# Where the conditioning sums stand in a feed-forward unit, and two attention turns moved among the value chunks

## The reference, cut to what matters

```python
def swiglu_ffn(x, w_in, w_out):                       # ffn1, ffn2, ffn3: hidden width 2816
    gate, up = jnp.split(x @ w_in, 2, axis=-1)
    return (jax.nn.silu(gate) * up) @ w_out

mod = c_act @ w_ada[i] + b_ada[i]                     # i = 0, 1; w_ada[i] is 1024 x 6144
sh_a, sc_a, g_a, sh_f, sc_f, g_f = jnp.split(mod, 6, axis=-1)

def _neighborhood_attention(h, w_qkv, rpb, w_o):      # 16 heads of 64, 4 rows of 64 columns
    q, k, v = ...                                     # h @ w_qkv
    s = jnp.einsum('bqhd,bkqjhd->bhqkj', q_r, k_g) + bias
    p = jax.nn.softmax(...)
    return jnp.einsum('bhqkj,bkqjhd->bqhd', p, v_g)   # then @ w_o
```

## Time and profile before

| | us |
|---|---|
| median of 3 runs | 1566.19 (1565.66 to 1570.25) |
| the profiled execution | 1566.99 |
| its span in the trace | 1565.2 |
| PE busy | 1511.3 (97%) |
| DVE busy | 1156.7 (74%) |
| ACT busy | 875.7 (56%) |
| POOL busy | 83.3 (5%) |

### The profile page before, as it was taken

One profiled execution on the slowest core, in us unless ns is written; L12 is line 12 of the kernel. 1 busy time (PEld: TensorE's weight loads), 2 busy tenths in 40 slices (PEclk: granted clock), 3 DMA queues, 4 the chain that ended last, 5 costly groups with the idle time before them and its releaser, 6 DMA issues.

```text
span 1565.2 us, 21487 instructions
## 1 busy us (share of the span) xinstructions
PE 1511.3 (97%) x8712; PEld 1256.7 (80%) x8712; DVE 1156.7 (74%) x1351; ACT 875.7 (56%) x1064; POOL 83.3 (5%) x90
## 2 busy tenths in 40 slices
PE   7999999989999999999999999999999999999998
PEld 6888879987778878967788876788888888888886
DVE  5767669765677767466767754579989888998997
ACT  5444457553534445365344444567777777777775
POOL 0100003220122200000000001000000000000000
PEclk9999999999999999999999999999999999999999
DMA  8887734222678764335877720359998998998993
GB/s 350 305 300 274 268 108 139 78 78 107 259 303 321 301 244 162 135 109 231 300 292 281 258 96 1 111 214 397 332 351 329 347 368 314 364 348 315 374 340 134
DMA packets 56788, 388.80 MB, mean 248 GB/s; under 512 B 10144, under 2 KB 10480, under 8 KB 12784
## 3 DMA queue, kind: packets, MB, share of 16 engines
q1 hardware_dynamic: 55280, 378.79, 64.4%
q0 software_dynamic: 1408, 8.60, 1.5%
HBM read 386.31 MB, written 1.06 MB: 247 GB/s over the span
## 4 chain that ended last, share of the span: by engine, by line
PE 85%; DVE 9%; ACT 4%; DMA 2%; issue 1%; DVEq 0%; ACTq 0%
PE bank L346 23%; PE bank L348 23%; PE bank L347 23%; PE bank L1369 4%; DVE sb_wlo L273 2%; DVE sb_ada_raw L786 2%; PE bank L1940 1%; DMA sb_ada_raw<-in_ada 1%; PE bank L591 1%; ACT sb_whi L269 1%; PE bank L748 1%; PE bank L2178 1%; PE bank L2140 1%; PE bank L2485 1%; PE bank L2519 1%
## 5 line engine op out<-in xcount | busy, mean ns | idle before, releaser
L273 DVE TENSOR_TENSOR sb_wlo<-sb_raw,sb_whi 128x2048 fp32r<-128x2048 f32 x135 | 311.4, 2308 | 114.5 <-ACT sb_whi L269 114.4
L269 ACT ACTIVATE sb_whi<-sb_raw 128x2048 fp32r<-128x2048 f32 x135 | 258.6, 1917 | 241.5 <-PE bank L348 227.5
L346 PE MATMUL bank<-sb_whi,sb_xhi 128*128 128x512 f32 (+1 forms) x736 | 280.5, 381 | 5.6 <-DVE sb_wlo L273 4.1
L347 PE MATMUL bank<-sb_wlo,sb_xhi 128*128 128x512 f32 (+1 forms) x736 | 275.6, 374 | 0.0
L348 PE MATMUL bank<-sb_whi,sb_xlo 128*128 128x512 f32 (+1 forms) x736 | 275.6, 374 | 0.0
L2449 DVE TENSOR_TENSOR sb_wlo<-sb_raw,sb_whi 128x2048 fp32r<-128x2048 f32 x84 | 190.9, 2286 | 12.6 <-ACT sb_whi L2443 11.9
L346 PE MATMUL bank<-sb_whi,sb_slots_hi 128*128 128x512 f32 x448 | 181.2, 404 | 0.0
L348 PE MATMUL bank<-sb_whi,sb_slots_lo 128*128 128x512 f32 x448 | 176.2, 393 | 0.0
L347 PE MATMUL bank<-sb_wlo,sb_slots_hi 128*128 128x512 f32 x448 | 175.5, 392 | 0.0
L2443 ACT ACTIVATE sb_whi<-sb_raw 128x2048 fp32r<-128x2048 f32 x84 | 160.9, 1917 | 25.5 <-PE bank L348 25.3
L346 PEld LDWEIGHTS bank<-sb_whi,sb_xhi 128*128 128x128 f32 x736 | 139.3, 189 | 33.1 <-DVE sb_wlo L273 6.2
(11 more groups left out here) (455 smaller groups left out, 2519.4 us busy)
## 6 DMA issues: line engine op xcount, KB each, us to landing
sb_raw<-in_ffn SPq DMA_DIRECT2D x98, 1024.0 KB, 5.8
sb_raw<-in_moe SPq DMA_DIRECT2D x86, 1024.0 KB, 6.4
sb_ada_raw<-in_ada SPq DMA_DIRECT2D x32, 1536.0 KB, 8.4
sb_cst<-in_moe SPq DMA_DIRECT2D x28, 1024.0 KB, 6.8
sb_xn<-in_moe SPq DMA_DIRECT2D x27, 1024.0 KB, 6.8
sb_ada_raw<-in_moe SPq DMA_DIRECT2D x27, 1024.0 KB, 6.7
sb_raw<-in_w_in SPq DMA_DIRECT2D x13, 1024.0 KB, 4.8
sb_raw<-in_na_qk SPq DMA_DIRECT2D x8, 1024.0 KB, 5.0
```

The costliest lines, as they stand in the source:

```text
L269: e.activation(whi[s][:, :], raw[s][:, :], ACT.Copy).then_inc(s_hi[s], 1)
L273: e.tensor_tensor(wlo[s][:, :], raw[s][:, :], whi[s][:, :], ALU.subtract).then_inc(s_lo[s], 1)
L346: e.matmul(dst, wh, xh, start=first, stop=False, skip_group_check=skip)
L347: e.matmul(dst, wh, xl, start=False, stop=False, skip_group_check=skip)
```

## The change

In `ffn`: the sums of piece j leave unit j and are made in unit j+1, one tile between `low` of B and `low` of A, two between `low` of A and `low` of C. On SP the transfer of piece j moves behind the loads of B and A. In the last units `low` of the last B chunk goes ahead of `v_hlo`, and the last piece of a feed-forward of 11 pieces is summed, all three tiles, behind its last `v_hlo`. In the attention, `attend` becomes a generator, and its turns 0 and 1 are taken behind value chunks 9 and 10; `meet` becomes `release` (no engine waits), the value products wait for all marks of `linear` instead, and the bank of the spread sums alternates the other way round (`turn`).

```diff
             def sp_unit(e, j):
                 if also is not None:
                     also(e, j)
+                load(e, B_, b0[B_] + j + 1, w[j + 1, 1])
+                load(e, A_, b0[A_] + j + 2, w[j + 2, 0])
                 if has_ada(j):
                     sp_ada(e, j)
-                load(e, B_, b0[B_] + j + 1, w[j + 1, 1])
-                load(e, A_, b0[A_] + j + 2, w[j + 2, 0])
                 load(e, C_, b0[C_] + j + 1, w[j + 1, 2])
@@ dve_unit
                 low(e, B_, b0[B_] + j)
+                if has_ada(j - 1):
+                    v_ada(e, j - 1, (0,))
                 low(e, A_, b0[A_] + j + 1)
-                if has_ada(j):
-                    v_ada(e, j, (0, 1))
+                if has_ada(j - 1):
+                    v_ada(e, j - 1, (1, 2))
                 low(e, C_, b0[C_] + j)
-                if has_ada(j):
-                    v_ada(e, j, (2,))
@@ sp_ffn
                 units(e, sp_unit)
+                load(e, B_, b0[B_] + n - 1, w[n - 1, 1])
+                load(e, A_, b0[A_] + n, w[n - 1, 2])
                 if has_ada(n - 2):
                     sp_ada(e, n - 2)
-                load(e, B_, b0[B_] + n - 1, w[n - 1, 1])
-                load(e, A_, b0[A_] + n, w[n - 1, 2])
                 if has_ada(n - 1):
                     sp_ada(e, n - 1)
@@ dve_ffn
-                if has_ada(0):
-                    v_ada(e, 0, range(ADA_T))
                 units(e, dve_unit)
                 dve_unit(e, n - 2)
...
+                    v_mult_rows(e, n - 2)
+                    low(e, B_, b0[B_] + n - 1)
+                    v_hlo(e, n - 2)
+                if has_ada(n - 2):
+                    v_ada(e, n - 2, (0,))
                 low(e, A_, b0[A_] + n)
+                if has_ada(n - 2):
+                    v_ada(e, n - 2, (1, 2))
                 (v_mult if rolled else v_mult_rows)(e, n - 1)
                 v_hlo(e, n - 1)
                 if has_ada(n - 1):
-                    v_ada(e, n - 1, (2,))
+                    v_ada(e, n - 1, range(ADA_T))
@@ attend
-    turn = lambda b, n: bank[b + n % 2][:, 0:T] if prepare is None else ...
+    turn = lambda b, n: bank[b + (n + b // 6) % 2][:, 0:T] if prepare is None else ...
@@ neighbourhood
+        def between():
+            calls.append(None)
+            if len(calls) in (2 * 9 + 2, 2 * 10 + 2):
+                next(turns)
```

More of the change, by code:

```diff
@@ L685, in ffn @@
                 tally["table"] += 1
-            has_ada = lambda j: isinstance(j, int) and j < ada_n
+            has_ada = lambda j: ada_n > 0 and isinstance(j, int) and j < ada_n
             def hbuf(j):
@@ L927, in dve_ffn @@
                 low(e, A_, b0[A_] + 1)
-                if has_ada(0):
-                    v_ada(e, 0, range(ADA_T))
                 units(e, dve_unit)
                 dve_unit(e, n - 2)
[L932 to L936, removed]
+                if rolled:
+                    v_mult(e, n - 2)
+                    v_hlo(e, n - 2)
+                    low(e, B_, b0[B_] + n - 1)
+                else:
+                    v_mult_rows(e, n - 2)
+                    low(e, B_, b0[B_] + n - 1)
+                    v_hlo(e, n - 2)
+                if has_ada(n - 2):
+                    v_ada(e, n - 2, (0,))
                 low(e, A_, b0[A_] + n)
+                if has_ada(n - 2):
+                    v_ada(e, n - 2, (1, 2))
                 (v_mult if rolled else v_mult_rows)(e, n - 1)
@@ L962, in ffn, with linear @@
             return acc
-        def linear(chunks, evac, parts, following, between=None, begin=ahead):
-            marks, done, slots = [], [], []
+        def linear(chunks, evac, parts, following, between=None, begin=ahead, marks=None):
+            marks, done, slots = [] if marks is None else marks, [], []
             n = len(chunks)
@@ L1917, in backwards, with attend, attend_turns @@
     return bass.AP(tensor=ap.tensor, offset=ap.offset + step * (n - 1), ap=[*ap.ap[:-1], [-step, n]])
-def attend(env, ctx, tag, scores, values, bias, m_ready, order=None, prepare=None):
+def attend(env, ctx, *args, **kw):
+    parts = []
+    for _ in attend_turns(env, ctx, parts, *args, **kw):
+        pass
+    return parts
+def attend_turns(env, ctx, parts, tag, scores, values, bias, m_ready, order=None, prepare=None, m_values=()):
     sb, bank, pe, act, dve = (env[n] for n in ("sb", "bank", "pe", "act", "dve"))
@@ L1997, in weigh @@
                     turn(4, n)[i % 2 * HD:(i % 2 + 1) * HD, :], values(i, kb), pt[i % 2][:, kb, :],
-                    start=kb == 0, stop=kb == NB - 1), m_pt[i], m_out.get(n - back))
+                    start=kb == 0, stop=kb == NB - 1), m_pt[i], m_out.get(n - back), *m_values)
     def scaled(n):
@@ L2004, in scaled @@
         m_out[n] = dve.step(lambda e: e.tensor_tensor(dst, b, a, ALU.mult), m_spread[n], m_pv[n])
-    parts = []
     for n in range(pairs + 2):
@@ L2032, in attend @@
             parts += env["split_pair"](at, m_out[at], m_out[at + 1])
-    return parts
+        yield
 def neighbourhood(env, early, m_in):
@@ L2088, in neighbourhood @@
         env["exp_table"]()
-        m1 = linear([(w, "channels") for w in ch["na_qk"]] + [(w, "tokens") for w in ch["na_v"]],
-                    lambda c, b, m: evac_qk(c, b, m) if c < 8 else evac_v(c - 8, b, m), m_in, ch["na_o"][:2])
-        meet()
+        m1, m, calls = [], [], []
         def scores(i, qb):
@@ L2095, in scores @@
             return q[hp:hp + HD, i // 2, qb * P:(qb + 1) * P], k[hp:hp + HD, i // 2, :]
+        turns = attend_turns(env, ctx, m, "na", scores, lambda i, kb: v[:, kb, i * HD:(i + 1) * HD], flat,
+                             lambda i: [m1[i // 4], m1[4 + i // 4], m_b[2 + i // 8, i % 8 // 2]],
+                             lambda z: backwards(z.rearrange("p (r c) -> p r c", c=GRID)), m_values=m1)
+        def between():
+            calls.append(None)
+            if len(calls) in (2 * 9 + 2, 2 * 10 + 2):
+                next(turns)
+        linear([(w, "channels") for w in ch["na_qk"]] + [(w, "tokens") for w in ch["na_v"]],
+               lambda c, b, m: evac_qk(c, b, m) if c < 8 else evac_v(c - 8, b, m), m_in, ch["na_o"][:2],
+               between=between, marks=m1)
+        env["release"]()
         spare = env["spare"]
         m_row, m_row2 = env["gate_rows"](0, spare[:, 0:D], spare[:, D:2 * D], *env["scratch_free"][0])
-        m = attend(env, ctx, "na", scores, lambda i, kb: v[:, kb, i * HD:(i + 1) * HD], flat,
-                   lambda i: [*m1, m_b[2 + i // 8, i % 8 // 2]],
-                   lambda z: backwards(z.rearrange("p (r c) -> p r c", c=GRID)))
+        for _ in turns:
+            pass
         env["release"]()
```

2 lines of the change are left out of this document (1 added, 1 removed).

## The result

The changed kernel takes 1573.17 us in the median (1571.27 to 1574.60, 9 runs), the kernel before on the same chip 1568.39 us (1564.07 to 1571.77, 9 runs). The ratio is 1.003 with a 95% interval of 1.0018 to 1.0042: it is slower by about 4.7 us, on the other side of the predicted 1.3 us of gain, and above the range. The profiled execution took 1574.6 us, its span is 1572.8; it is the slowest of the nine, so the two spans differ by 7.6 us where the medians differ by 4.8.

A forecast was written before the change was run, and what follows sets the result against it. Feed-forward changes pay only where PE waits, 8.0 us for h in seven waits. Terms: -1.2 +4.4 +1.4 (ffn1), -5.4 +5.3 (ffn2), -1.6 (attention), -3.2 -1.0 (ffn3) = -1.3, so 1564.9 us; range 1557 to 1572.

The forecast's parts named there:

- the attention: Turns taken between value chunks: PE pays only the work, 4.9 against 6.5 us; gain 1.6, bounds 0 and 3.
- The terms for ffn1, mixer, ffn2 and ffn3: Predicted stage changes: ffn1 +3.2, mixer +1.4 for the clock, ffn2 -0.1, ffn3 -4.2 us.
- The starts: Feed-forward starts: later sums remove PE's waits for h; gains 1.2 us in ffn1, 5.4 in ffn2, 3.2 in ffn3.
- the two terms -3.2 and -1.0: ffn3: 3.2 us gained at its start, 1.0 at its end by the earlier second remainder.
- The ends: Ends of ffn1 and ffn2: the last piece's late transfer delays the next stage, costing 4.4 and 5.3 us.
- rival 1: Ends of ffn1 and ffn2 cost nothing and gain 1.0 us each: 1551.8 us; chance 0.10.
- rival 2: Slow landings at both ends: from 9.2 us on the time passes 1570.9, at 13.5 it is 1579.3; chance 0.13.
- The clock: PE's half clock after idling: +1.4 us behind ffn1, nothing more behind ffn2; bounds 0 and 1.7 at each end.
- the likeliest case: Whole kernel within 0.3% (4.7 us) of the kernel before, neither faster nor slower; chance 0.65.
- Rival 3: Moved attention turns gain nothing and both feed-forward ends pay more clock, +1.6, +1.7, +0.3: 1568.5 us; chance 0.25.
- Rival 4: Waits at the feed-forward starts stay, costing back up to 9.8 us: 1574.7 us; chance 0.03.

The follow-up runs named there:

- e2: Kernel before with only the attention taken from the changed kernel; ratio 1.0016 to the kernel before.
- e1: Kernel before with only the feed-forwards taken from the changed kernel; ratio 1.0013 to the kernel before.
- e10: Changed kernel with the last but one piece summed ahead of the last output chunk's remainder, load order kept; one run, span 1559.3 us.
- e11: Kernel before with only `release` and swapped bank order, gate-row store held until turn 1's first exponentials; one run, span 1565.5 us.
- e3: Changed kernel with the store of the gate rows issued ahead of the q and k chunks; ratio 1.0006 to the kernel before.
- e6: Changed kernel with the store of the gate rows held until ACT is through the attention's fourth turn; one run, span 1567.5 us.
- e12: Kernel before with only `release` and swapped bank order, no turns between chunks, store not held; one run, span 1569.3 us.
- e8: Changed kernel with early gate-row store, sums moved gradually into DVE's idle time, last pieces loaded earlier; 1553.26 us, ratio 0.9902 to the kernel before.

## Why the prediction was wrong

The forecast failed in one step, the attention: -1.6 us predicted, +3.9 measured, 5.5 of the 8.9 us between the predicted sum (-1.3) and the change between the two spans (+7.6). The terms for ffn1, mixer, ffn2 and ffn3 are off by 2.0 us together (1.2 + 0.1 + 0.8 - 0.1), and 1.4 us lie outside the stages changed. By the medians the shares are alike: the attention's part costs 2.5 us (e2) where -1.6 was put, the feed-forwards' 2.0 (e1) where +0.3 was put, 4.1 and 1.7 us of a miss of 6.

**The starts: right.** All waits for h but 0.29 us are gone. In ffn3, where nothing lies against it, the two terms -3.2 and -1.0 met -4.3. The late B chunk is next there, as put: PE's wait for the remainder of h is 0.67 us at 760.64.

**The ends: right in their mechanism, sized 1 us too small each.** Issue, landing, chunk, three sums, remainder, addition came in the order and nearly at the times put; rival 1 fell. By the clock of the kernel before (0.93 us of later start taken off, 1.24 of gained start put back) the piece left at 191.0 (191.4 predicted), the first addition stood at 205.0 (204.4) and the second diagonal at 210.0 (204.69 + 4.4 = 209.1). The chunk came 3.2 us behind the piece in ffn1 and not 2.5 (in ffn2 it was 2.5), and the piece took 6.6 and 6.7 us and not 6.3; the slow landings of rival 2 (9.2 us and more) did not come. PE's idle time was put at 5.5 and 9 us and was 6.85 and 10.09, because the ends came about 1 us later than put and because the working left out that PE, which gains 1.0 us by the early remainder, also arrives sooner; this second part is idle time and no loss. e10 shows what the late piece cost: 4.3 us less in ffn1 and in ffn2 each.

**The clock: size right in this trace, but by chance.** +1.4 was put for ffn1's end and the mixer is +1.5. But in e1, whose half clock behind ffn1 lasts 10.2 us and not 6.8, the mixer takes 189.4 us, less than before: a stretch at half clock falls away later, at 232 to 236. In the kernel after, too, not all of it lies at ffn1's end: from there to the mixer's end it has 10.2 us more at half clock than before, 6.8 at 205.9 and 3.4 at 369.7. So the match of 1.4 and 1.5 does not show the term. Behind ffn2 nothing more was put, and the transposes with what follows took 6.07 us to the first product instead of 5.25. The Trainium skill (TensorE: Matmul & The Clock Gate, HAM oscillation) has a PE that waits for transfers start cold each time. The trace agrees behind ffn1 and ffn2 in the kernel after, and disagrees in e11: behind the very wait of 3.40 us that half clock followed in the kernel before, the clock stayed full and the 32 transposes took 4.11 us.

```profile
594.12 4.11 PE L591 MATMUL bank<-sb_sil,sb_ada_raw 128*128 128x128 f32 x32 [3.40 <-DVE sb_sil L535]
```

**The attention: the failed step.** "Between the chunks PE pays only the work" holds, and the gain is 1.8 us (e3 against e1; 1.0 in e6), where 1.6 was put. What the step left out is that the turns come earlier in ACT's program while the store of the gate rows does not move. The store ran beside turns 0 to 2 and the start of 3 before and harmed nothing; now it lies under turns 2 to 4, and at the third pair's sums ACT stands still until 9.59 us behind its issue. That the store has to be there is shown (e3, e6); by what it holds ACT is open. PE idles 2.3 us more (3.02 against 0.71 in e3) and is then busy 6.25 us at half clock, of which half is loss, 3.1; the stage as a whole is 4.8 us longer (136.0 in the kernel after against 131.2 in e3). The bounds of that term, 0 and 3 us of gain, reasoned only about what each engine does itself. A transfer that the change does not touch, but whose surroundings it moves, had no term, and no rival was of that kind. Without the standstill the time would have been e3's: 1568.66 us, ratio 1.0006, inside the range and within 0.3% as the likeliest case had it, though still 0.7 us above its kernel before (1567.99) and not 1.3 below.

Rival 3 rested on moved turns that gain nothing, and they gained 1.0 to 1.8 us; of its higher price for the clock 0.8 us came behind ffn2 (6.07 against 5.25). Rival 4 fell, the waits at the starts went.

## What to carry to other kernels

When a prefetch is moved a step later, look at the last step of the loop: there the lag meets the next stage's loads on one queue, and a transfer that leaves 4 us later there costs about what the starts gain (here 4.3 us in ffn1 and in ffn2, against gains put at 1.2 and 5.4). Spend the lag where the engine idles anyway, and switch over gradually, since the first use at the new place still has its transfer issued by the old one. When code moves past a small transfer with many tiny elements, count the transfer as a resource under it: it moves few bytes and can still hold up what is issued behind it, and here an engine beside it.

## What the runs showed of the hardware

- A store of 2048 elements of 4 bytes (8 KB) keeps transfers back for about 11 us: 1 MB chunks issued behind it landed after 15.7 us instead of 4.8, with the DMA engines at a share of 1.08 and 47 GB/s.
- The records of its packets lie in the first 3 us, yet the wait for it ends 10.9 us after its issue. The packets' times alone don't show how long it is in the way. The Trainium skill (DMA: Bandwidth & Descriptors, Why small descriptors are slow) gives each small packet a fixed overhead on top of its bytes; the trace agrees that such a transfer is slow for its bytes (8 KB in 10.9 us), and shows besides that its neighbours pay too.
- While such a store was under way ACT stood still with its inputs ready, until 9.3 to 10.1 us behind the store's issue (2.20 us in the kernel after, 1.90 to 2.69 in four others, 0.37 in e12). It did not in the kernel before, e1, e6 and e11.
- The same wait of 3.40 us behind ffn2 was followed by 3.4 us at half clock (before, e2, e8), by 6.8 around it (e12) and by none (e11). A stretch at half clock also moved from one place to another between kernels that are equal there. In these runs the length of a wait does not tell a clock term of 1 to 2 us.
